# One-hot expert groups moved in between dense score chunks, in a hybrid attention and product-key retrieval block

## The reference, cut to what matters

```python
def peer(h, w_q, sub_k1, sub_k2, u, v):          # 8 heads, 128 keys, top 16
    q = (h @ w_q).reshape(B, S, 8, 2, 128)
    s1 = einsum('bshd,nd->bshn', q[..., 0, :], sub_k1)
    s2 = einsum('bshd,nd->bshn', q[..., 1, :], sub_k2)
    v1, i1 = top_k(s1, 16);  v2, i2 = top_k(s2, 16)
    cand = v1[..., :, None] + v2[..., None, :]
    cidx = i1[..., :, None] * 128 + i2[..., None, :]
    sc, pos = top_k(cand, 16)
    eidx = take_along_axis(cidx, pos);  gate = softmax(sc)
    act = gelu(einsum('td,thkd->thk', h, u[eidx]))
    return einsum('thk,thkd->td', gate * act, v[eidx])
```

## Time and profile before

| | us |
|---|---|
| median of 3 runs | 1827.28 (1827.28 to 1831.05) |
| the profiled execution, its own time | 1828.94 |
| its span | 1827.1 |
| PE busy | 1672.7 (92%) |
| DVE busy | 1118.8 (61%) |
| POOL busy | 614.4 (34%) |
| ACT busy | 326.5 (18%) |

### The profile page before, as it was taken

One profiled execution on the slowest core, in us unless ns is written; L12 is line 12 of the kernel. 1 busy time (PEld: TensorE's weight loads), 2 busy tenths in 40 slices (PEclk: granted clock), 3 DMA queues, 4 the chain that ended last, 5 costly groups with the idle time before them and its releaser, 6 DMA issues.

```text
span 1827.1 us, 17662 instructions
## 1 busy us (share of the span) xinstructions
PE 1672.7 (92%) x6294; PEld 1088.2 (60%) x6294; DVE 1118.8 (61%) x2409; ACT 326.5 (18%) x857; POOL 614.4 (34%) x650
## 2 busy tenths in 40 slices
PE   6988999999998999999997996667999999999795
PEld 3454454455884888888886885556444444444342
DVE  0010444431219999999947567999666555566794
ACT  3002444340111021111111113554000000000032
POOL 0000345430002244333335443222545334444570
PEclk9988999999999999999998998777999999999897
DMA  6222111024446799999999998333999999999991
GB/s 205 80 93 93 57 36 35 12 90 144 139 146 199 254 344 373 362 357 378 344 369 349 409 409 319 112 115 100 401 409 409 409 409 409 409 410 409 408 348 54
DMA packets 131972, 475.56 MB, mean 260 GB/s; under 512 B 14716, under 2 KB 15740, under 8 KB 131885
## 3 DMA queue, kind: packets, MB, share of 16 engines
q0 software_dynamic: 73728, 268.47, 38.4%
q1 hardware_dynamic: 58156, 205.97, 30.2%
HBM read 471.19 MB, written 3.19 MB: 260 GB/s over the span
## 4 chain that ended last, share of the span: by engine, by line
PE 49%; DMA 30%; DVE 14%; issue 3%; POOL 2%; ACT 1%; SPq 1%; ACTq 0%; DVEq 0%; POOLq 0%
DMA arena<-in_v,eidx 21%; PE psum L1411 17%; DMA arena<-in_u,eidx 7%; PE psum L1319 6%; PE psum L1258 6%; PE psum L1148 5%; PE psum L1291 3%; PE psum L1279 3%; DVE arena L1011 3%; DVE arena L989 3%; DVE arena L1043 2%; DVE arena L1046 2%; DVE arena L1020 2%; PE psum L1216 2%; PE psum L1370 2%
## 5 line engine op out<-in xcount | busy, mean ns | idle before, releaser
L1411 PE MATMUL psum<-arena 128*128 128x256 f32 x2048 | 447.5, 382 | 13.3 <-issue 12.5
L484 POOL DMA_INDIRECT arena<-in_u,eidx x256 | 250.7, 979 | 595.3 <-DVE dots L989 369.0
L1429 PE MATMUL psum<-arena 128*128 128x512 f32 x1024 | 440.4, 592 | 2.2 <-DMA arena<-in_vd 1.4
L1411 PEld LDWEIGHTS psum<-arena 128*128 128x128 f32 x2048 | 391.6, 191 | 68.7 <-issue 14.0
L1011 DVE SCALAR_TENSOR_TENSOR arena<-arena,wts 128x1024 f32<-128x1024 f32 x254 | 323.3, 1285 | 175.2 <-DMA arena<-in_v,eidx 168.8
L484 POOL DMA_INDIRECT arena<-in_v,eidx x256 | 256.4, 1002 | 288.9 <-DVE arena L1011 233.0
L989 DVE CUSTOM_DVE_ANT_0 arena<-psum,arena 128x1024 f32<-128x1024 f32 x256 | 304.6, 1221 | 61.2 <-DMA arena<-in_u,eidx 50.8
L1429 PEld LDWEIGHTS psum<-arena 128*128 128x128 f32 x1024 | 194.2, 190 | 247.2 <-issue 243.0
L463 POOL TENSOR_SCALAR arena<-arena 128x256 f32<-128x256 f32 (+4 forms) x128 | 105.9, 846 | 281.5 <-DVE arena L767 223.9
L1422 PE MATMUL psum<-arena 128*128 128x128 f32 x512 | 100.7, 366 | 58.7 <-DVE arena L1046 36.5
L1422 PEld LDWEIGHTS psum<-arena 128*128 128x128 f32 x512 | 90.2, 266 | 69.3 <-DVE arena L1046 59.0
(11 more groups left out here) (167 smaller groups left out, 1274.4 us busy)
## 6 DMA issues: line engine op xcount, KB each, us to landing
arena<-in_ut SPq DMA_DIRECT2D x128, 512.0 KB
arena<-in_vd SPq DMA_DIRECT2D x128, 512.0 KB
arena<-in_wpack SPq DMA_DIRECT2D x105, 512.0 KB, 3.6
arena<-in_u,eidx POOLq DMA_INDIRECT x256
arena<-in_v,eidx POOLq DMA_INDIRECT x256
arena<-in_w_pg SPq DMA_DIRECT2D x8, 512.0 KB
arena<-in_x SPq DMA_DIRECT2D x4, 512.0 KB, 4.9
arena<-bias_rows SPq DMA_DIRECT2D x8, 256.0 KB, 5.6
```

The source lines that it names most:

```text
L484: G.indirect_dma_start(out=row_slot(n), out_offset=None, in_=a["v"] if values else a["u"], in_offset=bass.IndirectOffsetOnAxis(ap=eidx[:, ...
L1411: last = T.matmul(ps[6 + c % 2][:, 0:DT], u[:, k * P:(k + 1) * P], h2T1[:, k, :], start=(k == 0), stop=(k == KC - 1))
L1429: last = T.matmul(ps[BANK + 2 * t + h], mixed[:, c, t * P:(t + 1) * P], stream[:, c % SRING, h * HALF:(h + 1) * HALF], start=(c == 0), sto ...
```

## The change

1. The 64 one-hot groups run between dense chunks 62 to 125, one after each chunk, in 2 PSUM banks (`mix_bank`). The picks are transposed at chunk 59. A chunk's columns whose group was already made when the chunk comes (`groups_before`) are not in `mixed` as gelu: there ScalarE has copied the group's weights (`copy_mix`), the gelu goes to `late_gelu` (a ring of 4), and VectorE multiplies the two (`apply_late`). `apply_mix` covers only the chunks that are there already.
2. VectorE does 112 dots first, with all top work among them, and then two dots after each group.
3. Queries, key scores, their evacuation and `top_of_halves` go head by head for both tiles of a pair. `top_of_halves` of tiles 0 and 1 both come before the first numbers.
4. Each head's first eight picks are numbered among 20 candidates in two instruction groups of 4 heads (640 elements), the last eight among 50 in four groups of 2 heads (800 elements). The gathers take the columns in the order `PICK_ORDER`. 24 small copies at the start make the table of candidate numbers `candno`.
5. The one-hot buffers lie in `xs[:, 0:2, :]`, so all four tiles of `xs` are stashed in DRAM, and tiles 0 and 1 are loaded back after the groups. Both tiles' dot rows lie in PSUM (banks 0 to 3).

```diff
+LOW_RUNS = [(0, 1, 0, 8), (1, 1, 0, 4), (2, 2, 0, 2), (4, 4, 0, 1)]
+HIGH_RUNS = [(0, 1, 8, 16), (1, 1, 4, 8), (2, 1, 2, 5), (3, 1, 2, 4), (4, 1, 1, 3), (5, 3, 1, 2), (8, 8, 0, 1)]
+FIRST_MIX = 62
+TURN_AT = 59
+EARLY_DOTS = 112
+STEP_DOTS = 2
+LATE = 4
...
@@ SP
-                    for t in range(NG, TILES):
-                        sp.dma_start(xdram[t - NG, :, :], xs[:, t, :]).then_inc(rows_stashed, 16)
+                    for t in range(TILES):
+                        sp.dma_start(xdram[t, :, :], xs[:, t, :]).then_inc(rows_stashed, 16)
...
+                if i == CHUNKS + SRING - 1:
+                    sp.wait_ge(mix_made, WG)
+                    for t in range(NG):
+                        sp.dma_start(xs[:, t, :], xdram[t, :, :]).then_inc(rows_back, 16)
...
@@ gather
+                if n == 4 * 8:
+                    pool.wait_ge(experts_known, 3)
...
                 if values and k < SLOTS and n % SLOTS >= SLOTS - 2:
-                    pool.wait_ge(mix_made, WG)
+                    pool.wait_ge(dense_scores, CHUNKS)
...
@@ ScalarE
+            def dense_activate(c):
+                late = WGRP * groups_before(c)
+                sc = chunk_scores(c)
                 act.wait_ge(dense_scores, c + 1)
+                if late:
+                    if c - LATE > FIRST_MIX:
+                        act.wait_ge(late_applied, c - LATE - FIRST_MIX)
+                    last = A.activation(late_gelu[:, c % LATE, 0:late], sc[:, 0:late], ACT.Gelu_apprx_tanh)
+                if late < DT:
+                    last = A.activation(mixed[:, c, late:DT], sc[:, late:DT], ACT.Gelu_apprx_tanh)
+                last.then_inc(dense_gelu, 1)
...
+                g = c - FIRST_MIX
+                if 1 <= g <= WG:
+                    copy_mix(g - 1)
+                dense_activate(c)
+                if 0 <= g + 1 < WG:
+                    gate_hots(g + 1)
...
@@ VectorE
+            make_hots(0)
+            done = EARLY_DOTS
+            for s in range(WG + 1):
+                if s + 1 < WG:
+                    make_hots(s + 1)
+                if s >= 1:
+                    apply_late(FIRST_MIX + s - 1)
+                    apply_mix(s - 1)
+                more = min(done + STEP_DOTS, NG * COLS)
+                dots_until(done, more)
+                done = more
+            for c in range(FIRST_MIX + WG, CHUNKS):
+                apply_late(c)
+            dots_until(done, NG * COLS)
+            dve.wait_ge(rows_back, 16 * NG)
...
@@ TensorE
+            def scores(h, p):
+                pe.wait_ge(query_out, PH * h + p + 1)
+                if PH * h + p >= 2:
+                    pe.wait_ge(keyscores_out, 2 * (PH * h + p) - 2)
+                for t in range(2):
+                    for jj in range(2):
+                        last = T.matmul(ps[6 + p % 2][:, (2 * t + jj) * PK:(2 * t + jj + 1) * PK],
+                                        qT[:, 2 * p + jj, t * P:(t + 1) * P], pkeys[:, jj, :], start=True, stop=True)
+                last.then_inc(keyscores_ready, 1)
...
+            def mix(g):
+                pe.wait_ge(hot1_ready, g + 1)
+                pe.wait_ge(hot2_gated, g + 1)
+                if g < 2:
+                    pe.wait_ge(picks_out, 2)
+                else:
+                    pe.wait_ge(mix_applied, g - 1)
+                for j in range(WGRP):
+                    last = T.matmul(mix_bank(g)[:, j * P:(j + 1) * P], hot1[:, g % 2, j, :], hot2[:, g % 2, j, :],
+                                    start=True, stop=True)
+                last.then_inc(mix_made, 1)
...
                 last.then_inc(dense_scores, 1)
+                if 0 <= c - FIRST_MIX < WG:
+                    mix(c - FIRST_MIX)
 
             pe.wait_ge(dense_gelu, CHUNKS)
```

More of the change, by code:

```diff
@@ L173, in build @@
         s12_0, _ = place(2048, [2 * PH, PK])
+        s12_1, _ = place(4096, [2 * PH, PK])
         qT, _ = place(8192, [2 * PH, HT])
@@ L186, in build @@
         scr = hn[0]
-        assert ra == 100 * DT
-        vals, ra = place(ra, [2 * PH, TK])
-        idxu, ra = place(ra, [2 * PH, TK], u32)
+        vals, idxu = [None] * 2, [None] * 2
+        for par in range(2):
+            vals[par], ra = place(ra, [2 * PH, TK])
+            idxu[par], ra = place(ra, [2 * PH, TK], u32)
         idxf, ra = place(ra, [2 * PH, TK])
@@ L697, in _ @@
             V.memset(rbias[0:HEADS, 2 * P - 1:S + P], NEG).then_inc(bias_rows_out, 1)
+            dve.wait_ge(pool_consts_set, 6)
+            off = 0
+            for a0, na, b0, b1 in LOW_RUNS + HIGH_RUNS:
+                for x in range(na):
+                    start = ROW_START[a0 + x]
+                    V.tensor_copy(candno[:, off:off + b1 - b0], iota[:, start + b0:start + b1])
+                    off += b1 - b0
             dve.wait_ge(rms_ready, 1)
@@ L854, in top_of_halves, with pair_up @@
                 after(last)
-                for j in range(j0, j1):
-                    last = V.max_index(idxu[:, j, 8:16], vals[:, j, 8:16], rest[:, j - j0, :])
+                for v, i, sc, j, r in rows:
+                    last = V.max_index(i[:, j, 8:16], v[:, j, 8:16], rest[:, r, :])
                 after(last)
-                if t and j1 == 2 * PH:
-                    dve.sem_inc(halves_done, 1)
-            def pair_up():
-                after(V.tensor_copy(idxf, idxu))
+            def pair_up(t):
+                after(V.tensor_copy(idxf, idxu[t % 2]))
@@ new lines, in dots_until @@
+            def dots_until(n0, n1):
+                for n in range(n0, n1):
+                    dot(*divmod(n, COLS))
+            for k in range(EARLY_DOTS):
+                dot(0, k)
+                step, off = divmod(k, 4)
+                if off == 2 and step < 5:
+                    later_top(1, step)
+                if off == 2 and 5 <= step < 13:
+                    top_of_halves(1, step - 5)
+                if off == 2 and 13 <= step < 18:
+                    later_top(2, step - 13)
+                if off == 2 and 18 <= step < 23:
+                    later_top(3, step - 18)
+                if k == 40:
@@ L1071, in _ @@
-            for g in range(WG):
-                make_hots(g)
-                if g >= 2:
-                    apply_mix(g - 2)
-                if g % W_STEP == W_STEP - 1:
-                    dot(1, W_AT + g // W_STEP)
-            apply_mix(WG - 2)
-            apply_mix(WG - 1)
-            for k in range(W_AT + WG // W_STEP, COLS):
-                dot(1, k)
+            dve.wait_ge(rows_stashed, 16 * TILES)
+            make_hots(0)
[9 more added lines that the diff above has]
+                done = more
```

339 lines of the change are left out of this document (167 added, 172 removed).

## The result

The changed kernel takes 1726.24 us (1725.47 to 1727.63), against 1827.28 us before: a ratio of 0.9445, 95% interval 0.9429 to 0.9461, 5.5% faster. The prediction was 1734 (1720 to 1764).

The account below looks back on a forecast made before the run. It took dense scores as bound by TensorE, groups by VectorE, then TensorE and transfers both full. From 1827.1 us, -112.9 for earlier values, +17.9 given back and +2 for bursts made 1734.1, so 1734 us (1720 to 1764).

Parts of the forecast that it names:

- The bound, and what replaces it: Group stage, 1122 to 1272 us: bound by VectorE; once mixed with dense chunks, TensorE sets the pace, VectorE close behind.
- The step: Mixed stage: TensorE needs 3.457 us for a chunk and 0.92 for a group, 4.375 us a step.
- Values start: End of the mixed stage: values can start at 1161.0 us instead of 1273.9, a gain of 112.9 us.
- The start: Before the first norm: 24 small copies on VectorE delay it by 1.2 us (0 to 2).
- VectorE up to the picks: Before chunk 59: VectorE's last gates come at 846 us, TensorE arrives at 862 and does not wait, margin 16 us.
- the 868 of the rival: At chunk 59: with top work at its old length the picks come at 868 us, costing 6 us; chance 0.06.
- What is given back: Value stage: twelve gathers more and two loads of `xs`, 14 transfers of 1.28 us each, cost 17.9 us.
- The 2 us for bursts: Added to the sum for small waits of TensorE behind bursts of gathers.
- the round robin: Skill rule for DMA queues: the stream would get half, 205 GB/s, without stalls, making the 2 us added for bursts 0.
- Hand-overs: Mixed stage rival: waits between engines make a step 4.7 us, late ones 4.9, adding 26 us to 1760; chance 0.16.
- gather issue: Mixed stage rival: POOL needs 4.5 us a step to issue two gathers, adding 7 us to 1741; chance 0.04.
- serial step: Mixed stage rival: a group's path does not overlap with the chunk, 7.77 us a step, 1951 us; chance 0.04.

Follow-up runs that it names:

- e3: The changed kernel with one dot instead of two after each group; 1833.76 us.
- e5: The changed kernel with one buffer for the one-hot rows instead of two; 1750.17 us, ratio 0.9518 to the kernel before.
- e4: The changed kernel with three dots instead of two after each group; 1747.77 us.
- e2: The changed kernel with all picks numbered among 50 candidates, two heads at a time; 1746.27 us, ratio 0.9534 to the kernel before.
- c4: The changed kernel with gathers 99 to 118 waiting for dense chunks, candidate-table copies behind the first norm and eight more dots in the steps; 1714.08 us, ratio 0.9379.
- c1: The changed kernel itself, run again as a control; 1725.69 us, ratio 0.9445 to the kernel before.
- e8: The changed kernel with candidate-table copies behind the first norm, 118 early dots instead of 112 and extra dots in some steps; 1739.36 us, ratio 0.9452.
- e1: The changed kernel with all groups put back behind the dense chunks; 1942.01 us, ratio 1.0599 to the kernel before.
- e7: The changed kernel with the 24 candidate-table copies behind the first norm instead of ahead of it; 1745.21 us, ratio 0.9501 to the kernel before.
- c3: The changed kernel with all groups behind the dense chunks and gathers 99 to 231 waiting for dense chunks; 1821.03 us, ratio 0.9962 to the kernel before.
- c2: The changed kernel with gathers 99 to 118 each issued only when a given dense chunk is done; 1725.93 us, ratio 0.9448 to the kernel before.
- e6: The changed kernel with 118 early dots instead of 112; 1749.70 us, ratio 0.9509 to the kernel before.

## Why the prediction was right, step by step

- **The bound, and what replaces it.** Right. The group stage was VectorE's and idle for the rest; in the mixed stage TensorE sets the pace. e3 (less VectorE work, same 274.89 us), e5 (less slack, same 274.89) and e4 (more VectorE work, 5.12 us a step with waits for DVE) show this from three sides.
- **The step.** 4.375 us predicted, 4.35 measured, from 0.90 instead of 0.92 for the group: 1.6 us in all.
- **Values start.** 1161.0 predicted, 1156.23 measured. The start was +2.8 instead of +1.2. The front behind it was mis-sized the other way: dense chunks at 654.97 instead of 657.9, outside the 656 to 660 that I had named as a sign of being right. I had kept the 11.46 us between the end of `project_out(1)` and the second norm's transposes but for 0.5; it shrank to 9.2. VectorE, done with tile 0's pairs earlier, now adds the mixer's first banks while TensorE still projects (first addition at 575.55, the projection ends at 578.10). Before, the first addition began only when the projection had ended, 544.88 + 27.75:

```profile
575.55 0.69 DVE L871 TENSOR_TENSOR arena<-arena,psum 128x512 f32<-128x512 f32 x1 [2.05 <-PE psum L1380]
587.25 3.56 PE L1393 MATMUL psum<-ident,arena 128*128 128x128 f32 x16 [9.16 <-DVE arena L878]
```

  The first pair ended 1.0 sooner behind its start than I took (550.62 against 548.8 + 2.8), and the second cost 1.5 less.
- **VectorE up to the picks.** 846 predicted for the last gates, 843.6 measured, because the dots began at 598.8 and not 601; the 245 us from there are right to 0.2. TensorE reached chunk 59 at 858.8: a margin of 15 us, where I had 16. e2 used it up and then waited, at the 868 worked out for it. Two smaller figures of the prediction don't come out of their terms: 54.9 less 2 x 9.87 less 24.7 plus 17.5 plus 0.6 is 28.6 us a tile and not 27.7, and the 868 of the rival is 22 us beyond 846 and not 13. Neither moves the forecast, since the margin covers the first and 868 is the figure used.
- **What is given back.** +17.9 predicted. From the values' start to the last accumulate the time grew from 518.7 to 536.6, by the 17.9; behind it the tail, which I had called unchanged, was 1.5 shorter (34.5 and 33.0), so that the whole is +16.4. When the values ended 63 accumulates were left, as predicted. The price of 1.28 us a gather is confirmed by e3, c4 and, at 1.23, e4.
- **The 2 us for bursts, and their cause.** Not there in the changed kernel's trace or in c1, but 10 to 23 us in e3 and e5 to e8. Here the prediction misread the trace of before. It took 11.7 us of lost TensorE time at 978 to 1001 for a stream that the gathers crowd out. In that trace too the gelus of the chunks that end at 979.06 and 984.51 come at 991.62 and 1000.11, 12.6 and 15.6 us late, SP issues with them, and all that it had issued before 991 had landed by 986.8:

```profile
991.62 0.38 ACT L646 ACTIVATE arena<-psum 128x256 f32<-128x256 f32 x1 [10.95 <-remote]
1000.11 0.38 ACT L646 ACTIVATE arena<-psum 128x256 f32<-128x256 f32 x1 [8.10 <-remote]
```

  So the rows are no case of two full queues, and the round robin that the prediction set them against is neither borne out nor refuted by them. The loss itself is real, comes in some executions and not in others, and was underrated: e1 lost over 130 us to it. In the mixed stage no trace has it, as the prediction said, though it said so because of the transfers. That none of the changed kernel's nine runs shows it (1725.46 to 1727.63) is in part luck: in e5 and e7, with as many early dots, it cost 11 to 15 us.
- **The sum.** 8 us too high, in three parts: 4.8 at the values' start (+1.6 at the start, -4.5 in the front behind it, -1.8 from the first chunk on), 1.5 in the tail and the 2 for bursts.
- **Hand-overs, gather issue, serial step.** None came. POOL's issues in the mixed stage took 1.07 us on average (134.19 us for 125; median 0.94, longest 1.45), less than 3 us a step. The Trainium skill (SBUF — State Buffer, SBUF: two separate sides) has GpSimd locked out while VectorE holds the shared port pair; the step of over 6.2 us that I estimated from its figures did not come beside VectorE's one-hot and multiply instructions. Whether the issues above 0.94 us are short waits of this kind no run shows.

**Open.** Why TensorE's signals come late, and why in one execution and not in another of the same instructions; whether unbroken dots, the gathers behind them or both are needed for it; whether e1 would have it on the chip of c3. In the tails of e2, e3 and e5 to e8 VectorE stood for 4 to 12 us for TensorE's transposes, which had ended 3 to 11 us before it went on; the first trace, e1, e4 and c1 to c4 have none of it. No run looked into that.

## What to carry to other kernels

When one stage is full on one engine and the next on another, put a slice of the one behind each slice of the other, and check three sums per step: the engine that sets the pace, the second fullest with its growth over the stage, and the transfers. Then price what the shorter stage no longer hides; here every gather left over cost 1.28 us of saturated transfer. Where gathers and a stream share the transfers, breaking up a long run of gathers and their consumers, by other work between them or by a wait on the stream's progress, cost nothing here (c2) and every kernel that was paced, c2 to c4, was free of the stall (as was c1 without it). And when one queue has nearly all of the transfers, look at when the other's blocks were issued and when they landed before calling it starved: here they had landed, and the next ones had not been asked for.

## What the runs showed that I had not expected

- TensorE's signals can come up to 45 us late in the trace, and what then shows first is a DMA split: 44.73 against 3.66 MB in e1 (880 to 1000 us), 9.56 against 1.14 in e6, while c3 had 28.12 against 18.09 in the same stretch as e1, which is all that its chunks use (151 GB/s). The Trainium skill (DMA: Bandwidth & Descriptors, Queues, rings and completion order), by which the engines alternate between queues that have work, packet by packet, is no guide to such a split, since the stream's queue had no work for most of the time.
- Tiny copies on VectorE follow each other every 0.06 us, less than half of the 0.139 of the instructions of 50 elements, and inside the 0.05 to 0.09 that I took from them.
- The mixed stage repeated to the hundredth of a microsecond, 274.89 us, in eight kernels (the changed one, e3, e5 to e8, c2, c4) on three chips or more; e2's took 274.97. A stage bound by TensorE alone is a good ruler for what else has changed.
